# Second pass of a pooling and RWKV-7 trunk: projections of two blocks in one product, and part of the head moved into the inverse

## The chip, the cores and the metric

The kernel runs on one core of a Trainium2 chip. The metric is the device time of one execution in microseconds (us). The median of three executions of the kernel before is 2558.65 us, between 2556.53 and 2560.04.

## What is computed

The reference takes `x` of 4096 tokens by 1024 channels in float32 and one conditioning vector. Cut to what matters here:

```python
u = rms_norm(h, norm_gain) * (1 + scale) + shift
proj = u @ w_in                       # pool value, pool gate, r, k, v, w_down, a_down, rwkv gate
pf = p + (token_shift(p) - p) * mu    # on r | k | v | w_down | a_down
w_log = -softplus(-(w0 + tanh(wd) @ w_lora_up)) - 0.5;  decay = exp(-exp(w_log))
a = sigmoid(a0 + ad @ a_lora_up)
kk = l2_normalised(k * k_k);  k = k * (1 + (a - 1) * k_a)
# for each token, per head of 64 channels:
state = state * w_t + (state @ a_t) b_t^T + v_t k_t^T;  y_t = state @ r_t
y = group_norm(y) + (r * k * r_k).sum() * v
h = h + gate * (concat(y_pool * silu(...), y * silu(rg)) @ w_out)
out = rms_norm(h) * final_gain
```

The recurrence over tokens is what makes the second half of the kernel: tokens are taken in blocks, and inside a block the recurrence becomes products of small matrices and the inverse of a triangular one.

## The kernel before

All data are float32. A first pass computes the pooling branch and writes the transposed, normalised input to memory (`xt_dram`). The second pass, which the change touches, computes the RWKV branch in 32 blocks (`N2`) of 128 tokens (`T2`), each of two chunks of 64 tokens. A loop takes two blocks at a time (`each_block`, blocks 2 to 29), blocks 0 and 1 stand before it and 30 and 31 behind it.

**Queues.** Nothing is scheduled by a planner: each engine has its own queue, written out by hand in `run` (VectorE, ScalarE, GpSimd, SyncE) and in `front` and `back` (TensorE). Every engine works its queue strictly in order, and waits are on semaphores that count up per block.

**Projection.** The input of a block, `xT`, is 8 tiles of 128 channels by 128 tokens. 17 column tiles of weights are multiplied with it: tile 12 (low rank inputs), 0 to 3 (r), 4 to 7 (k), 8 to 11 (v), and 13 to 16 (the gate). Each tile takes 8 accumulated products (a float32 product shows as two records of MATMUL). They are put in five groups (`GROUPS`), which use PSUM banks 0 and 1 in turn. ScalarE copies a group out, scaled by `mu`, into `prev` (`take_group`, L1470), VectorE combines it with the bank to `mix` (`shift`, L1713), and only then may TensorE start the group after the next, which is what `mix_ready` tells it.

**Fillers.** The products of block n+1 are not run in a row: `project` is cut into 34 slots of four products, and `fill(k)` in `back` puts k slots of them between the small products of block n, so that TensorE has work while VectorE and ScalarE handle what the small ones gave. Inside the inverse (`inverses`, steps 0 to 5, L1276 and L1279) they use the full width of 128 weight columns (L1221). From step 5 on they are put as two halves of 64 columns (`halves`, L1202). The last six slots stand at the end of the block.

**The block's own work.** `front(n)` makes the variance of block n-1, the bonus, transposed values (L1364) and keys (`BT`, L1377), and the Gram matrices (L1386), for which it waits for VectorE's `LA` (L1851, L1857). Then `back(n)`: six slots, the inverse with the output product of block n-1 in two halves (L1256), and twice `from_state` (L1308), VectorE's copy `R` (L1793), `solve` (L1319), ScalarE's copy `UV`, and `state_and_output` (L1332, L1340, L1341). Behind the first of these VectorE sums the state (`stmp`, L1799) and makes the new one (`SV`, L1805).

**The head of block n+1** (low rank products L1232, sigmoid, key norm, decays `egi`, `sig`, `egx`, and `BK`) is worked behind the inverse of block n, between the state products, since its tiles are projected during that block.

**Loads.** SyncE issues for each block n: the load of `xT` for block n+2 (after the gate group of block n has been projected), the store of block n-1's output after `final_norm` (L1785), and, once that store has landed, the load of block n's residual rows (`gate_row`).

## Time and profile before

| | |
|---|---|
| median of three executions | 2558.65 us (2556.53 to 2560.04) |
| profiled execution | 2556.52 us, of which the core's span is 2553.4 us |
| TensorE busy, share of the span | 2484.1 us, 97% |
| VectorE, ScalarE, GpSimd busy | 65%, 45%, 17% |
| granted TensorE clock, mean | 0.988 |
| second pass | from about 659 us to the end |

Busy shares are of the whole span. A MATMUL's own duration includes its way through the array and overlaps with the next one; what a product costs in a row of products is therefore read from the distance between starts. An instruction's idle time is what its engine stood still before it, with the one that ended it.

### The profile page before, as it was taken

To read this page: it belongs to the slowest core of one execution; us is meant where nothing else is said; L and a number is where in the kernel's file an instruction comes from. 1 tells how busy PE (TensorE), PEld (TensorE's weight loads), DVE (VectorE), ACT (ScalarE), POOL (GpSimd) and SP (SyncE) were. 2 spreads that over 40 slices of the span, in tenths; PEclk is the share of its full clock that TensorE was granted. 3 is DMA by queue.
4 is the path that set the end of the run, shared out by engine and by line. 5 is a ranking of instruction groups with operands and counts; after the bars stand their busy time and mean duration, and the time that the engine had idled before them with its cause. 6 is when DMAs were issued, how large, how long until landed. Compare 5 with 4: busy or idle time off the path is not lost.

```text
span 2553.4 us, 73693 instructions
## 1 busy us (share of the span) xinstructions
PE 2484.1 (97%) x30485; PEld 2052.2 (80%) x30485; DVE 1660.4 (65%) x3462; ACT 1146.2 (45%) x2539; POOL 427.3 (17%) x565
## 2 busy tenths in 40 slices
PE   6999999999999999999999999999999999999995
PEld 6867776677678888888888888888888888888883
DVE  5653343433367777777777777677777776777774
ACT  4423322231235545444555545445555454455552
POOL 4211101111022111211111112111111111111110
PEclk8999999999999999999999999999999999999997
DMA  8513333126310100000100000000101000001000
GB/s 325 154 70 109 118 131 131 45 103 217 130 51 27 35 26 27 26 27 26 38 32 28 34 27 26 27 26 32 38 27 35 27 26 27 26 27 43 27 19 26
DMA packets 72618, 152.91 MB, mean 60 GB/s; under 512 B 3801, under 2 KB 38190, under 8 KB 71342
## 3 DMA queue, kind: packets, MB, share of 16 engines
q1 hardware_dynamic: 69918, 143.71, 16.0%
q8 instruction: 231, 3.78, 0.6%
q10 hardware_dynamic: 2448, 5.24, 0.6%
q14 instruction: 21, 0.17, 0.0%
HBM read 98.61 MB, written 50.33 MB: 58 GB/s over the span
## 4 chain that ended last, share of the span: by engine, by line
PE 85%; DVE 8%; ACT 4%; issue 3%; DVEq 0%; DMA 0%; SPq 0%; ACTq 0%
PE banks L1221 21%; PE banks L386 15%; PE banks L1202 13%; PE banks L1256 9%; PE banks L482 9%; PE banks L1276 7%; DVE SM L1868 2%; PE banks L1332 1%; PE banks L1386 1%; PE banks L1319 1%; PE banks L380 1%; PE banks L1340 1%; PE banks L1341 1%; PE banks L1308 1%; DVE t L1753 1%
## 5 line engine op out<-in xcount | busy, mean ns | idle before, releaser
L1221 PE MATMUL banks<-xT,wts 128*128 128x128 f32 x5232 | 633.7, 279 | 0.0
L1221 PEld LDWEIGHTS banks<-xT,wts 128*128 128x128 f32 x5232 | 598.3, 192 | 30.9 <-issue 27.1
L1531 ACT ACTIVATE LX<-banks 128x512 f32<-128x512 f32 (+1 forms) x384 | 184.9, 524 | 642.4 <-DVE WT L1812 436.3
L1202 PE MATMUL banks<-xT,wts 128*64 128x128 f32 x6944 | 420.1, 274 | 0.0
L1202 PEld LDWEIGHTS banks<-xT,wts 128*64 128x64 f32 x6944 | 380.2, 137 | 6.3
L1648 POOL TENSOR_TENSOR BK<-k,egi 64x512 f32<-64x512 f32 x64 | 96.3, 1504 | 928.3 <-ACT egi L1500 888.5
L1256 PE MATMUL banks<-wo,Y 128*128 128x512 f32 x512 | 232.9, 598 | 4.7 <-DVE Y L1772 4.7
L386 PE MATMUL banks<-ts,wts 128*128 128x256 f32 x1024 | 231.5, 379 | 0.0
L1812 DVE TENSOR_TENSOR WT<-banks,level_mask 128x256 f32<-128x256 f32 x256 | 102.5, 422 | 194.2 <-PE banks L1276 186.2
L482 PE MATMUL banks<-wo,yc 128*128 128x512 f32 x512 | 223.3, 595 | 0.0
L386 PEld LDWEIGHTS banks<-ts,wts 128*128 128x128 f32 x1024 | 194.9, 190 | 26.6
L482 PEld LDWEIGHTS banks<-wo,yc 128*128 128x128 f32 x512 | 96.8, 191 | 117.8 <-issue 117.7
L386 PE MATMUL banks<-xT,wts 128*128 128x256 f32 x768 | 180.1, 383 | 2.0 <-ACT xT L587 2.0
L1637 POOL TENSOR_TENSOR LA<-SM,ones 64x256 f32<-64x256 f32 x128 | 93.5, 730 | 529.3 <-DVE Y L1772 515.4
L1470 ACT ACTIVATE prev<-banks,vec 128x128 f32<-128x128 f32 x416 | 121.4, 374 | 121.9 <-PE banks L1221 114.1
L1256 PEld LDWEIGHTS banks<-wo,Y 128*128 128x128 f32 x512 | 93.5, 193 | 99.8 <-issue 94.3
L386 PEld LDWEIGHTS banks<-xT,wts 128*128 128x128 f32 x768 | 147.0, 192 | 26.2 <-issue 3.3
L1276 PEld LDWEIGHTS banks<-LX,W 64*64 64x64 f32 x4096 | 111.9, 134 | 58.0 <-issue 50.3
L1276 PE MATMUL banks<-LX,W 64*64 64x128 f32 x4096 | 143.1, 278 | 2.5 <-ACT LX L1531 1.5
L1713 DVE SCALAR_TENSOR_TENSOR mix<-banks,omu,prev 128x128 f32<-128x128 f32 x416 | 119.3, 345 | 26.0 <-ACT prev L1470 8.6
L873 DVE TENSOR_TENSOR fgain<-banks,fgain 128x256 f32<-128x256 f32 x96 | 40.7, 424 | 128.2 <-PE banks L386 127.4
L1840 DVE STREAM_TRANSPOSE WL<-banks 32x128 f32<-32x128 f32 x128 | 39.8, 311 | 126.8 <-PE banks L1276 123.8
(194 smaller groups left out, 3742.6 us busy)
## 6 DMA issues: line engine op xcount, KB each, us to landing
wo<-in_x SPq DMA_DIRECT2D x8, 2048.0 KB, 9.5
xt_dram<-xT SPq DMA_DIRECT2D x32, 512.0 KB, 8.4
xr<-in_x SPq DMA_DIRECT2D x32, 512.0 KB, 5.7
h_dram<-xr SPq DMA_DIRECT2D x32, 512.0 KB, 2.7
xT<-xt_dram SPq DMA_DIRECT2D x32, 512.0 KB, 3.4
gate_row<-h_dram SPq DMA_DIRECT2D x32, 512.0 KB, 3.4
out<-gate_row SPq DMA_DIRECT2D x32, 512.0 KB, 2.6
wts<-in_w_in SPq DMA_DIRECT2D x4, 2048.0 KB, 8.4
```

The lines of the kernel that those rows point to most:

```text
L386: last = nc.tensor.matmul(product_ps(g, i), w1[:, g, left, k], right[:, k], start=(k == 0), stop=(k == KH - 1))
L482: last = nc.tensor.matmul(bank[BANK_OUT[h]][:, :], yc[:, k, j * P:(j + 1) * P], wo1[:, k, h * 512:(h + 1) * 512], start=(k == 0), stop=(k ...
L1202: last = nc.tensor.matmul(o[half(c)], lhsT[:, half(c)], rhs, start=start, stop=stop)
L1221: last = (by_halves if halves else nc.tensor.matmul)(bank[b][:, q * P:(q + 1) * P], w2_tile(k, t0 + q), xT[par][:, k, :], start=(k == 0), ...
L1256: last = nc.tensor.matmul(bank[(4, 7)[h]][:, :], Y[:, p], wo2[:, p, h * 512:(h + 1) * 512], start=(p == 0), stop=(p == NP - 1))
L1276: last = nc.tensor.matmul(step_banks[a][half(c), j, p * P:(p + 1) * P], W[h, a, j, p], (LX if i else AI)[h, a, j, p].rearrange(flat), star ...
L1470: nx(nc.scalar.activation(prev[:, t, 1:], src, ACT.Copy, scale=v("mu", t)), mix_in, hold=False)
L1531: s(nc.scalar.activation(to, of, ACT.Copy), lx_ready, hold=False)
L1637: return nc.gpsimd.tensor_tensor(to, of, one, ALU.mult)
L1648: hd(nc.gpsimd.tensor_tensor(BK[h, :, :, 1 - e], chunks(k2[h]), chunks(egi[h]), ALU.mult), kt_ready if e else head_pool)
L1713: ins = nc.vector.scalar_tensor_tensor(out=mix[:, t], in0=bank[b][:, q * P:(q + 1) * P], scalar=omu[:, t:t + 1], in1=prev[:, t, 0:T2], op0 ...
L1812: s(nc.vector.tensor_tensor(WT[:, a], left(a)[:, :, 0:2, 0], mask_of(level_mask[i]), ALU.mult), wt_ready, hold=False)
```

## The change

Blocks are numbered as above; "an even block's projection" is the one that runs during the odd block before it.

- `xT` holds two blocks side by side, and the 13 tiles that go through `mix` are projected for two neighbouring blocks at once, 256 columns per product. Tiles 12, 4 to 9 are taken for blocks (2k+1, 2k+2) while block 2k runs; tiles 10, 0 to 3 and 11 for (2k, 2k+1) while block 2k-1 runs. The gate tiles stay at 128 columns. A group has at most two such tiles. Slots are now two products of 256 columns, or four of 128 for the gate: 36 and 32 slots.
- `fill(7)` stands where `fill(6)` stood.
- `prev` keeps only the two groups in flight. The last column of each tile is carried over in `carry` by small copies of ScalarE (three per group), and GpSimd's copy of that column goes.
- For even blocks, the low rank products, the key norm, the sigmoids and the decays move inside the inverse of the odd block before (`low_rank(0, (4, 7))`, `tanh`, `key(0)`, `clamp`, `decay_sum`, `taken_key`), and the final norm of the block before moves to the end of the odd block.
- `decay_ahead` and the exponential for `egx` go: `decay` has a leading column of ones, and serves both left sides. `dend` is copied from it.
- `xT` is loaded in two halves, each to rows of 512 bytes in SBUF that are 1024 bytes apart, where one load filled rows of 4096 bytes.
- The prologue projects the seven tiles of block 0 at 128 columns and the six others for blocks 0 and 1; block 31's seven are projected alone, at 128 columns.

```diff
-            GROUPS = [(12, 1, 0), (0, 4, 1), (4, 4, 0), (8, 4, 1), (13, 4, 0)]
+            GROUPS = ([(10, 1, 0), (0, 2, 1), (2, 2, 0), (11, 1, 1), (13, 4, 0)],
+                      [(12, 1, 0), (4, 2, 1), (6, 2, 0), (8, 2, 1), (13, 4, 0)])
+            GATE = 4
...
-                    sp.dma_start(xT[par][:, :, :], rows_of(xt, n)).then_inc(xT_loaded[par], 16)
+                    for h in range(2):
+                        k = slice(h * KH, (h + 1) * KH)
+                        sp.dma_start(xT[:, k, par, :], rows_of(xt, n)[:, k]).then_inc(xT_loaded[par][h], 16)
...
+                                for h in range(2):
+                                    pe.wait_ge(xT_loaded[par][h], (n - par) * 8 + 16)
+                                if seg is None:
+                                    pe.wait_ge(xT_loaded[1 - par][0], (n + par) * 8 + 16)
...
-                    fill(6)
+                    fill(7)
                     s.wait(bt_ready, 2)
-                    inverses(fill, (lambda h: None) if first else out_half, first)
+                    ahead_of = ahead and par == 1
+                    inverses(fill, (lambda: low_rank(0, (4, 7))) if ahead_of else (lambda: None),
+                             (lambda h: None) if first else (lambda h: out_half(h, ahead_of)), first)
+                    if ahead_of:
+                        key_norm()
                     from_state(0, first)
-                    if ahead:
-                        low_rank()
+                    if ahead and not ahead_of:
+                        low_rank(1)
...
+                    before, col = prev[:, b], carry[:, t0:t0 + w]
...
+                    nc.scalar.activation(before[:, 0:w, f, 0:1], col.unsqueeze(2), ACT.Copy)
                     for q in range(w):
-                        src = bank[b][:, q * P:(q + 1) * P]
-                        t = t0 + q
-                        nx(nc.scalar.activation(prev[:, t, 1:], src, ACT.Copy, scale=v("mu", t)), mix_in, hold=False)
+                        to, of = (before[:, q, :, 1:], both(b, q)) if seg is None else (before[:, q, seg, 1:], both(b, q, seg))
+                        ins = nc.scalar.activation(to, of, ACT.Copy, scale=v("mu", t0 + q))
+                    nx(ins, taken)
...
                     s.wait(y_ps, 1)
                     new_state(0, s, s_ready)
+                    if odd:
+                        decay_sum()
+                    if even:
+                        shift(n + 1, 1 - par, 2, seg)
+                    take_r(1)
+                    if odd:
+                        new_key(1)
+                    if even:
+                        new_key(0)
+                    state_sum(1)
+                    if even:
+                        decayed_key()
+                        if not first:
+                            final_norm(n - 1)
+                    if odd:
+                        taken_key()
                     if ahead:
-                        decay_sum()
-                    take_r(1)
+                        shift(n + 1, 1 - par, 3, seg)
```

(In the code `even` and `odd` speak of the block n+1 whose head is worked: `even` is true while an odd block runs.)

**TensorE, behind the inverse of an odd block.** Before, all blocks alike: step 5, a filler, `from_state` (L1308), low rank (L1232), `solve` (L1319).

```order
L1279 MATMUL banks<-LX,WL 64x64 x7
L1202 MATMUL banks<-xT,wts 64x128 x8
L1308 MATMUL banks<-SV,LA 64x64 [waits sv_ready,carried_ready,bt_ready,la_ready,lx_ready]
L1308 MATMUL banks<-SV,LA 64x64 x7
L1232 MATMUL banks<-th,up 128x128 [waits th_ready,mix_ready]
L1232 MATMUL banks<-mix,up 128x128
...
L1319 MATMUL banks<-R,LX 64x64 [waits r_ready]
L1319 MATMUL banks<-R,LX 64x64 x7
L1202 MATMUL banks<-xT,wts 64x128 x16
```

Now, in odd blocks:

```order
L1316 MATMUL banks<-LX,WL 64x64 x7
L1211 MATMUL banks<-xT,wts 64x256 x4
L1211 MATMUL banks<-rn,head_sum 64x512 [waits kk2_ready,lx_ready]
L1211 MATMUL banks<-rn,head_sum 64x512
L1347 MATMUL banks<-SV,LA 64x64 [waits sv_ready,bt_ready,carried_ready,la_ready]
L1347 MATMUL banks<-SV,LA 64x64 x7
L1358 MATMUL banks<-R,LX 64x64 [waits r_ready]
L1358 MATMUL banks<-R,LX 64x64 x7
L1211 MATMUL banks<-xT,wts 64x256 x8
```

The key norm stands ahead of `from_state` and the low rank products are gone from here, so `solve` follows `from_state` directly.

**TensorE, between the two chunks of an odd block, now.** The gate group opens the fillers behind the first `state_and_output` (L1380 is its last product).

```order
L1380 MATMUL banks<-LA,SV 64x64
L1211 MATMUL banks<-xT,wts 64x128 [waits mix_ready]
L1211 MATMUL banks<-xT,wts 64x128 x15
L1347 MATMUL banks<-SV,LA 64x64 [waits s_ready,v1_ready,la_ready]
L1347 MATMUL banks<-SV,LA 64x64 x7
```

Before, the fillers at this place needed no wait, and the gate group began two stops later, behind the second `solve`:

```order
L1202 MATMUL banks<-xT,wts 64x128 x16
L1202 MATMUL banks<-rn,head_sum 64x512 [waits kk2_ready]
L1202 MATMUL banks<-rn,head_sum 64x512
L1308 MATMUL banks<-SV,LA 64x64 [waits s_ready,v1_ready,la_ready]
L1308 MATMUL banks<-SV,LA 64x64 x7
L1202 MATMUL banks<-xT,wts 64x128 x8
L1319 MATMUL banks<-R,LX 64x64 [waits r_ready]
L1319 MATMUL banks<-R,LX 64x64 x7
L1202 MATMUL banks<-xT,wts 64x128 [waits mix_ready]
```

The gate group's wait has moved ahead of the second `from_state`.

**VectorE, the end of an odd block, now.** The first `mix` here is `shift(n + 1, ..., 2)`, the gate group's `mix_ready`; `gate_row` is the final norm of block n-1, after which its output may be stored.

```order
L1883 TENSOR_TENSOR stmp<-banks,SV 64x256 [waits s_ps,head_dve]
...
L1889 TENSOR_TENSOR SV<-stmp,dend 64x256 [waits y_ps,dve2_own]
...
L1800 SCALAR_TENSOR_TENSOR mix<-banks,omu,prev 128x256 [waits mix_in]
...
L1877 COPY R<-banks 128x256 [waits r_ps,mix_ready]
...
L1844 TENSOR_TENSOR BK<-rn,egi 64x8x64 [waits exps_ready,sum_ready]
L1844 TENSOR_TENSOR BK<-rn,egi 64x8x64
L1869 SCALAR_TENSOR_TENSOR gate_row<-gate_row,hstat,fgain 128x1024 [waits hn_ready]
...
L1800 SCALAR_TENSOR_TENSOR mix<-banks,omu,prev 128x256 [waits mix_in]
...
L1935 TENSOR_TENSOR LA<-mix,decay 64x8x64 [waits exps_ready,y_ps]
```

The same stretch before, without a final norm, which stood behind the first `R` and `rgate`:

```order
L1799 TENSOR_TENSOR stmp<-banks,SV 64x256 [waits s_ps,rk_ready]
...
L1752 TENSOR_TENSOR kk<-kk,rn 128x512 [waits rn_ready,sum_ready]
...
L1753 SCALAR_TENSOR_TENSOR t<-kk,sig 128x512 [waits head_dve]
...
L1713 SCALAR_TENSOR_TENSOR mix<-banks,omu,prev 128x128 [waits mix_in]
L1713 SCALAR_TENSOR_TENSOR mix<-banks,omu,prev 128x128 x3
...
L1760 TENSOR_TENSOR BK<-t,egi 64x8x64 [waits exps_ready]
L1760 TENSOR_TENSOR BK<-t,egi 64x8x64
...
L1851 TENSOR_TENSOR LA<-mix,sig 64x8x64 [waits exps_ready,y_ps]
```

The key work (`kk`, `t`) has left the end of the odd block and the final norm has come to it; `shift` of group 2 has come in behind the new state.

## Rows read from the trace of the kernel before

**Rows 1.** Stretches: length, busy us (count) of PE, PEld, DVE, ACT, POOL, clock, DMA

```profile
1000.00:2000.00 1000.00, 991.37 (x15244) 852.09 (x15240) 739.75 (x1635) 509.32 (x1196) 160.79 (x197) 1.00 0.09 29
```

**Rows 2.** Timeline of PE, one block: start, us, line, operation, count, idle before

```profile
1521.74 5.62 PE L1221 MATMUL banks<-xT,wts 128*128 128x128 f32 x48
...
1536.59 2.94 PE L1221 MATMUL banks<-xT,wts 128*128 128x128 f32 x24
1539.37 3.60 PE L1256 MATMUL banks<-wo,Y 128*128 128x512 f32 x8
...
1578.87 5.62 PE L1221 MATMUL banks<-xT,wts 128*128 128x128 f32 x48
```

**Rows 3.** Timeline of PE in the first pass, products of 256 columns

```profile
304.26 5.34 PE L386 MATMUL banks<-ts,wts 128*128 128x256 f32 x24
309.44 1.89 PE L386 MATMUL banks<-xT,wts 128*128 128x256 f32 x8
```

**Rows 4.** Timelines of PE, of DVE and of ACT, from inverse to state

```profile
1555.38 0.37 PE L1232 MATMUL banks<-th,up 64*128 64x128 f32 x1
...
1559.10 0.69 PE L1332 MATMUL banks<-UV,BT 128*64 128x64 f32 x16
...
1555.49 0.42 DVE L1793 COPY R<-banks 128x256 f32<-128x256 f32 x1 [1.72 <-PE banks L1308]
...
1561.47 0.87 DVE L1805 TENSOR_TENSOR SV<-stmp,dend 64x256 f32<-64x256 f32 x2
...
1556.16 1.14 ACT L1470 ACTIVATE prev<-banks,vec 128x128 f32<-128x128 f32 x4
...
1558.58 0.38 ACT L1536 ACTIVATE UV<-banks 64x256 f32<-64x256 f32 x1
```

**Rows 5.** Groups by form, 1000 to 2000 us: count, busy us, mean ns, idle

```profile
L1713 DVE SCALAR_TENSOR_TENSOR mix<-banks,omu,prev 128x128 f32<-128x128 f32 x226 | 64.9, 345 | 8.8
...
L1517 ACT ACTIVATE hstat<-hstat 128x1 f32<-128x1 f32 x17 | 3.4, 203 | 0.5
```

**Rows 6.** Timelines of DVE, then of PE, across a block's end

```profile
1498.92 1.28 DVE L1785 SCALAR_TENSOR_TENSOR gate_row<-gate_row,hstat,fgain 128x1024 f32<-128x1024 f32 x1 [0.15 <-ACT hstat L1517]
...
1510.65 0.88 DVE L1799 TENSOR_TENSOR stmp<-banks,SV 64x256 f32<-64x256 f32 x2 [0.23 <-PE banks L1332]
...
1512.29 1.66 DVE L1753 SCALAR_TENSOR_TENSOR t<-kk,sig 128x512 f32<-128x512 f32 x1
...
1518.21 1.41 DVE L1857 TENSOR_TENSOR LA<-kk,egx 64x512 f32<-64x512 f32 x2
...
1511.29 5.46 PE L1202 MATMUL banks<-xT,wts 128*64 128x128 f32 x96
1516.54 1.08 PE L1202 MATMUL banks<-rs,head_mean 128*64 128x512 f32 x4
...
1519.78 2.03 PE L1386 MATMUL banks<-LA,BK 64*128 64x128 f32 x32
```

**Rows 7.** Timeline of SyncE's queue

```profile
1500.36 0.36 SPq L1172 DMA_DIRECT2D out<-gate_row  x1
1504.54 0.33 SPq L1181 DMA_DIRECT2D gate_row<-h_dram  x1
...
1557.67 0.36 SPq L1172 DMA_DIRECT2D out<-gate_row  x1
1560.52 0.33 SPq L1181 DMA_DIRECT2D gate_row<-h_dram  x1
```

**Rows 8.** Issues of DMAs: KB each, median us to landing

```profile
xT<-xt_dram SPq DMA_DIRECT2D x32, 512.0 KB, 3.4
...
u<-in_pool_w ACTq DMA_DIRECT2D x1, 256.0 KB, 3.0
```

**Rows 9.** Timeline of PE: prologue of the second pass, and block 31

```profile
659.34 30.53 PE L1221 MATMUL banks<-xT,wts 128*128 128x128 f32 x272
...
2496.45 1.99 PE L1276 MATMUL banks<-AI,W 64*64 64x128 f32 x32 [5.45 <-DVE W L1824]
```

More of the change, by code:

```diff
@@ L1412, in back @@
                     fill(2, halves=True)
-                    if ahead:
+                    if ahead and not ahead_of:
                         key_norm()
@@ L1598, in run @@
                     take_y(0)
[L1599 removed]
+                    if odd:
                         sigmoid(1)
```

328 lines of the change are left out of this document (203 added, 125 removed).

## The prediction, made before the result was known

> **What bounds the kernel now.** I read the page's busy shares first, then the busy time by stretch, then TensorE's timeline over one block. TensorE is busy 97% of the span and 991.37 of 1000 us in the middle of the second pass, at full clock [rows 1]. The block shown lasts 57.13 us, 1521.74 to 1578.87 [rows 2]; the 17.5 blocks in those 1000 us share 8.6 us without work, 0.5 each. So time can be won only where TensorE's own work gets shorter, and any wait that is put before TensorE is paid in full. VectorE and ScalarE have idle time, but their chains of steps end exactly when TensorE asks for them: its Gram products begin at 1519.78, when the second `LA` ends at 1518.21 + 1.41 = 1519.62 [rows 6], and the state product begins at 1559.10, 0.14 us after the last `UV` [rows 4]. There is no slack that a new wait could use up.
>
> **What the wide product gives.** Distances of starts: full width at 128 columns, 1536.59 to 1539.37 for 24 records, 0.1158 us each. Two halves of 64 at 128 columns, 1511.29 to 1516.54 for 96, 0.0547 each, so 0.1094 for a pair [rows 2, 6]. At 256 columns, 304.26 to 309.44 for 24, 0.2158 [rows 3]. Twice 128 costs 0.2316 at full width and 0.2188 in halves. So a wide record saves 0.0158 at full width, nearly nothing in halves. No row shows halves at 256; I take 0.108 (half of 0.2158), between 0.107 and 0.109.
>
> Per pair of blocks before: 320 full-width records (20 of 34 slots per block), 37.06 us, and 448 half ones, 24.51: 61.57. After, 21 slots of each block are at full width and all are wide: 168 x 0.2158 = 36.25. In halves remain 8 gate slots per block, 256 x 0.0547 = 14.00, and 3 and 7 wide slots, 80 x 0.108 = 8.64. Sum 58.89, so **2.7 us less per pair**, and this is all that TensorE gains: the small products are the same in number.
>
> The Trainium skill (TensorE: Matmul & The Clock Gate, Back-to-back issue gap) gives N/2.4 + 2.5 ns for a warm gap, so hardly any gain from a wider product. With two passes over the columns for float32 it fits rows 3 (215.8) and the pairs of halves (109.2), but at full width and 128 columns the row has 115.8. By the page the gain per pair would be some 0.5 us and not 2.7, 32 us more over the kernel; the row of before decides.
>
> **What the new order puts before TensorE**, per pair of blocks.
>
> (a) *`solve` in odd blocks.* Low rank, 16 records from 1555.38 on, covers VectorE's `R` today. It moves away and nothing comes in its place. `R` ended at 1555.49 + 0.42 = 1555.91, 0.53 after `from_state`, and a release takes 0.14 (`UV` to L1332) [rows 4]. TensorE waits **0.7**.
>
> (b) *The gate group in odd blocks.* It opens the fillers right behind the first `state_and_output`, on the bank of group 2, so it waits for `mix_ready` of `shift(2)`. VectorE's queue has that behind the new state `SV`, which waits for `y_ps`, the end of the same `state_and_output`. TensorE stands for 0.11 (from its last product to VectorE's start, 1555.38 to 1555.49), 0.87 for `SV` [rows 4], two shifts and 0.14. A shift at 256 columns is not in the trace. Bounds are 0.345 at 128 and twice that; `R`, 256 columns from PSUM, takes 0.42 [rows 4, 5] and is nearest. I take 0.9 for two: **2.0** (1.8 to 2.5). The next product behind it, `from_state`, has what it needs by then, so nothing is given back.
>
> (c) *`xT` for the even block's run.* An even block's first filler now reads the load for the block two ahead as well. In SyncE's queue that load is behind the store of block n-1, which in odd blocks waits for a final norm moved to the block's end, and behind the residual load, which waits for that store to land. Count from the final norm's end, T. The store is issued 0.16 later (1498.92 + 1.28 to 1500.36), the residual load 2.85 or 4.18 after that [rows 6, 7], the first half of `xT` 0.4 later, at T + 3.4. An `xT` load of 512 KB lands 3.4 after its issue, one of 256 KB from elsewhere 3.0 [rows 8]; the residual load has 512 KB too. Landing is between T + 6.4 and, behind the residual's bytes, T + 7.7. TensorE asks at T + 5.7: shift 0.5, both `LA` (two like the row's, with gaps) 2.9, Gram products 1.96, gaps 0.3 [rows 2, 6]. Wait 0.7 to 2.0; I take **1.2**. The second half is asked for 1.7 later and lands in that time. What would cover it is nothing, since the slots ahead of the inverse all need this input. The load in rows of 512 bytes is not in the trace in this direction.
>
> The Trainium skill (DMA: Bandwidth & Descriptors, Anatomy of one DMA) has 2.0 us + bytes/436 KB per us, so 2.6 for a half, and 3.2 for 512 KB where the trace has 3.4; by it alone (c) would be 0.3 and the sum 14 us less.
>
> (d) *The end of odd blocks.* Six slots (1511.29 to 1516.54, 5.25) cover VectorE's chain from the end of `stmp` (1511.53) to that of the second `LA` (1519.62), 8.1 us. Now three gate slots, 2.6. The chain loses `kk` and `t`, which fill it up to 1513.95 (2.4), and some 0.6 of `mix`, and gains a final norm of 1.3: about 6.4. Filler shorter by 2.6, chain by 1.7: **0.8** (0.5 to 1.0) before bonus or Gram products [rows 6].
>
> (e) *ScalarE.* Before `UV` in even blocks ScalarE copied four tiles in 1.14 us [rows 4]. Now it makes two copies of 256 columns, the same columns in all with two fewer starts, some 0.9, and three small ones of 0.2 [rows 5]: 1.6. The state product followed `UV` by its release time, so it comes **0.5** later. In odd blocks the decays stand before the last step's copy, for which the key norm waits: **0.3**.
>
> Moving `tanh`, `clamp`, `key`, `decay_sum` into the inverse costs nothing: VectorE idles there under the output products and wide fillers. The dropped `egx`, its exponential, and GpSimd's carry shorten chains that only (d) reads.
>
> Sum per pair: 0.7 + 2.0 + 1.2 + 0.8 + 0.8 = 5.5 lost, 2.7 won, **+2.8**. The wide projections run in 15 pairs: +42 us.
>
> **Ends.** The prologue took 30.5 us for 272 records, 0.112 each [rows 9]. It gets 11 tiles at 128 columns (176 records, 19.7) and 6 at 256 (96, 20.7): +9.9, in the open. Block 30 then projects 6 tiles fewer (11.1 us of work), but its inverse is short of fillers; block 31, with none, stands 5.45 us before step 0 [rows 9]. I give back 4 (0 to 9). Together +6.
>
> **Sum.** 2556.52 (profiled) + 42 + 6 = 2604.5. The median of before is 2.1 above its profiled execution, so about **2605 us**, ratio 1.018.
>
> **Rivals.**
> - *The load is in time* (c = 0). For it: it may overlap the residual's. Against: the store must land first, which is 2.85 at least. 2605 - 18 = 2587.
> - *The load is much later*: 4.18 to the residual load or slow 512-byte rows, 2 us more per pair: 2635. One of three such distances seen in rows 7 and behind them was 4.18.
> - *Break-even*: (c), (d), (e) nearly nil, only (a) and (b) remain, which equal the gain: 2558 + 6 = 2564, or a little less.
> - *Faster*: the gate group does not wait. That needs `shift(2)` to be done before the fillers behind `state_and_output`; then VectorE is also 0.9 earlier for what follows, and (b), (d) vanish. With (a), (e), (c) at their low ends, 2.0 lost against 2.7, and the ends' 6 outweighed only if block 30 gives back 9: 2548. If all waits hid, 2556.5 - 40 + 6 = 2523. It decides at 2.3 us of waits per pair. Against it is the queue's order, in which `y_ps` stands ahead of that shift.
>
> **Chances.** Forecast 0.50 (2590 to 2622), load in time 0.18, load much later 0.12, break-even 0.08, faster 0.12. A difference of 0.2% (5 us) is about what can be told from no change. Slower by over 0.2%: 0.82; within: 0.06; faster: 0.12. The range 2560 to 2636 leaves out the faster case and the far end of the late load.
>
> **What would show it.** Starts of full-width wide records 0.216 apart. In odd blocks, TensorE idle some 0.7 before `solve` and some 2 before the first gate product, the releaser a `mix` of VectorE. In even blocks, idle before the first filler with a DMA or nothing named; a period of two blocks near 116.8 where it was 114.0, odd blocks longer than even ones in their middle. The forecast is wrong if TensorE is still 99% busy in the middle, if the gate product starts within 0.5 us of the state products, or if the pair is under 114.

## The result

The changed kernel takes **2674.47 us** (median of 5 runs, 2671.70 to 2686.11), the kernel before 2558.65 in the same comparison (5 runs). The ratio is 1.0472, 95% interval 1.0457 to 1.0486: slower by 116 us. The forecast was 2605 with a range of 2560 to 2636. The direction was right, the size was not: 46 us of loss were forecast, 2.5 times as much came.

The profiled execution of the changed kernel took 2686.11 us, with a span of 2684.4 and a mean granted clock of 0.971; it is the longest of the five, and the other four were granted 0.975 or 0.976. Its line numbers have moved: full-width fillers are L1251, fillers in halves and all other products by halves L1211, steps of the inverse L1313, the state product L1371, the Gram products L1425, VectorE's shift L1800.

The middle of the second pass, in the view that [rows 1] show for before (length, busy us and counts of PE, PEld, DVE, ACT, POOL, granted clock, DMA):

```profile
1000.00:2000.00 1000.00, 944.45 (x12108) 736.26 (x12109) 668.61 (x1394) 483.76 (x1212) 143.17 (x161) 0.98 0.08 27
```

TensorE is busy for 944 us where it was for 991, and the granted clock is 0.98 where it was 1.00. A clock that moved is the first thing for which the prediction had no term. TensorE's waits between 700 and 2600 us (total us, times, longest):

```profile
PE banks L1211 <- DVE mix L1800: 36.4, 26, 2.0
PE banks L1251 <- DMA xT<-xt_dram: 35.5, 15, 3.6
PE banks L1425 <- DVE LA L1940: 16.1, 16, 1.1
PE banks L1358 <- DVE R L1877: 10.3, 15, 0.7
PE banks L1371 <- ACT UV L1598: 5.2, 15, 1.0
```

All five were forecast by name, and four of them come once in each pair of blocks. The `mix` row holds two: the gate group's, 2.03 us in 15 pairs, and the bonus product's, 0.5 to 0.7 us in 11 of them. Together they are 6.8 us per pair.

TensorE's timeline, first an undisturbed run of fillers, then an odd block from the gate group on and the start of the next even block's run of fillers (start, us, in brackets the idle time before it and who ended it):

```profile
1530.94 6.31 PE L1251 MATMUL banks<-xT,wts 128*128 128x256 f32 x28
1537.19 1.10 PE L1313 MATMUL banks<-AI,W 64*64 64x128 f32 x32
...
1573.14 3.11 PE L1211 MATMUL banks<-xT,wts 128*64 128x128 f32 x32 [2.03 <-DVE mix L1800]
1576.03 1.07 PE L1347 MATMUL banks<-SV,LA 128*64 128x64 f32 x16
...
1578.63 1.97 PE L1211 MATMUL banks<-xT,wts 128*64 128x128 f32 x32
...
1586.07 1.09 PE L1211 MATMUL banks<-sig,rk_sum 128*64 128x128 f32 x16 [0.55 <-DVE mix L1800]
...
1589.50 2.06 PE L1425 MATMUL banks<-LA,BK 64*128 64x128 f32 x32 [1.06 <-DVE LA L1940]
1594.15 7.97 PE L1251 MATMUL banks<-xT,wts 128*128 128x256 f32 x28 [2.59 <-DMA xT<-xt_dram]
```

Not only the waits count here. The 32 records behind the gate group's wait need 2.89 us to the next product, where 32 such records at full clock need 1.80. The 28 wide records behind the load's wait need 7.90 (1594.15 to 1602.05), where the same 28 undisturbed need 6.25 (1530.94 to 1537.19). The stretches behind the two waits show why; the number behind POOL is the granted clock:

```profile
1574.00:1576.00 2.00, 2.00 (x22) 2.00 (x20) 0.00 (x0) 0.00 (x0) 0.00 (x0) 0.50 0.00 0
...
1594.00:1595.00 1.00, 0.85 (x2) 0.73 (x3) 0.88 (x2) 0.00 (x0) 0.00 (x0) 0.64 0.01 3
1595.00:1597.00 2.00, 2.00 (x6) 1.62 (x5) 1.90 (x6) 0.00 (x0) 0.00 (x0) 0.50 0.00 0
```

After standing still for 2.03 and for 2.59 us TensorE works at 0.50, which is 1.2 GHz, for some 3 us, and then again at 2.4 GHz. It does not follow every such wait, and that gives the price within one execution. The same place two pairs of blocks earlier, behind a wait of the same 2.03 us, with the granted clock at 1.00:

```profile
1329.60 1.97 PE L1211 MATMUL banks<-xT,wts 128*64 128x128 f32 x32 [2.03 <-DVE mix L1800]
...
1333.45 1.97 PE L1211 MATMUL banks<-xT,wts 128*64 128x128 f32 x32
...
1330.00:1333.00 3.00, 3.00 (x66) 2.83 (x64) 0.81 (x3) 0.00 (x0) 0.00 (x0) 1.00 0.00 0
```

From the gate group's first product to the second chunk's fillers it is 3.85 us here and 5.49 there (1573.14 to 1578.63): the lower clock costs 1.64. Behind the load's wait it costs as much: 7.90 for the run of 28, and 6.21 for the one behind a wait of 2.31 us at which the clock stayed up (1838.38 to 1844.59). In this execution the clock fell behind 13 of the 15 gate group's waits and 13 of the 15 load's waits (1.9 to 3.6 us).

From the first Gram products of block 1 to those of block 30 a pair takes 121.96 us (before 114.03, forecast 116.8). Block 0's Gram products begin at 742.30, before at 727.18. So the steady part lost 115 us, the prologue 15 and block 0 and the last two blocks together about 1, which is the difference of the spans, 131.

### The profile page after: what moved, and what is told of

Its sections match the earlier page's. It is cut to its first block, busy times and chain, and to the rows that moved or that the text cites. A ratio compares the mean times of both kernels' runs of the same rounds, so it can differ in the third digit from the quotient of the medians.

```text
span 2684.4 us, 65522 instructions
## 1 busy us (share of the span) xinstructions
PE 2517.2 (94%) x26409; PEld 1940.3 (72%) x26409; DVE 1624.5 (61%) x3229; ACT 1152.8 (43%) x2694; POOL 421.5 (16%) x534
## 4 chain that ended last, share of the span: by engine, by line
PE 84%; DMA 5%; DVE 5%; ACT 4%; issue 2%; SPq 1%; POOL 0%; DVEq 0%; ACTq 0%; POOLq 0%
PE banks L1251 24%; PE banks L386 15%; PE banks L1211 13%; PE banks L1293 8%; PE banks L482 8%; PE banks L1313 6%; DMA xT<-xt_dram 2%; DMA out<-gate_row 1%; PE banks L1371 1%; PE banks L1358 1%; PE banks L1425 1%; PE banks L1347 1%; DMA xT<-in_w_ada 1%; DVE BK L1844 1%; PE banks L1379 1%
## 5 line engine op out<-in xcount | busy, mean ns | idle before, releaser
L1251 PE MATMUL banks<-xT,wts 128*128 128x256 f32 (+1 forms) x2876 | 668.3, 387 | 38.5 <-DMA xT<-xt_dram 35.5
L1251 PEld LDWEIGHTS banks<-xT,wts 128*128 128x128 f32 x2876 | 529.7, 197 | 135.5 <-issue 65.2
L1211 PE MATMUL banks<-xT,wts 128*64 128x128 f32 (+1 forms) x5224 | 406.5, 308 | 30.4 <-DVE mix L1800 30.4
L1211 PEld LDWEIGHTS banks<-xT,wts 128*64 128x64 f32 x5224 | 320.3, 142 | 63.2 <-DVE mix L1800 32.5
L386 PEld LDWEIGHTS banks<-xT,wts 128*128 128x128 f32 x768 | 147.4, 192 | 26.3 <-issue 3.3
L1313 PEld LDWEIGHTS banks<-LX,W 64*64 64x64 f32 x4096 | 112.0, 134 | 68.1 <-issue 66.1
L1313 PE MATMUL banks<-LX,W 64*64 64x128 f32 x4096 | 143.2, 278 | 2.5 <-ACT LX L1593 1.6
L1524 ACT ACTIVATE prev<-carry 128x2 f32<-128x2 f32 (+1 forms) x132 | 28.1, 213 | 258.0 <-PE banks L1251 223.6
L1908 DVE STREAM_TRANSPOSE W<-WT 128x256 f32<-128x256 f32 x320 | 121.7, 418 | 0.0
L1800 DVE SCALAR_TENSOR_TENSOR mix<-banks,omu,prev 128x256 f32<-128x256 f32 (+1 forms) x215 | 94.6, 472 | 37.6 <-ACT prev L1530 15.7
```

The lines of the kernel that those rows point to most:

```text
L386: last = nc.tensor.matmul(product_ps(g, i), w1[:, g, left, k], right[:, k], start=(k == 0), stop=(k == KH - 1))
L1211: last = nc.tensor.matmul(o[half(c)], lhsT[:, half(c)], rhs, start=start, stop=stop)
L1251: last = one(to, w2_tile(k, t0 + q), x, start=(k == 0), stop=(k == KT - 1))
L1313: last = nc.tensor.matmul(step_banks[a][half(c), j, p * P:(p + 1) * P], W[h, a, j, p], (LX if i else AI)[h, a, j, p].rearrange(flat), star ...
L1800: ins = nc.vector.scalar_tensor_tensor(out=mix[:, t, of], in0=both(b, q)[:, of], scalar=omu[:, t:t + 1], in1=prev[:, b, q, of, 0:T2], op0= ...
L1908: s(nc.vector.transpose(W[:, a].rearrange("p j q t -> p (j q t)"), WT[:, a].rearrange("p j q t -> p (j q t)")), w_ready, hold=False)
```

## The experiments

Theory A: the changed kernel loses by the waits in TensorE's queue that its new order makes, and by a granted clock that falls behind the two long ones. Rivals: each product costs more than it did (the width, or the traffic beside it); TensorE is slow after a wait for another reason than the clock; or the load is slow in itself. Every ratio is against the kernel before on the same chip in the same comparison. Differences between two versions are differences of medians, mostly from two comparisons; the kernel before had medians between 2554.7 and 2558.65 in them, so such a difference is good to about 4 us.

### The gate group's shift earlier

Odd blocks only; on VectorE the shift stands ahead of the state's sum and not behind the new state:

```diff
                     elif ahead:
                         shift(n + 1, 1 - par, 2, seg)
...
+                    if even:
+                        shift(n + 1, 1 - par, 2, seg)
                     state_sum(0)
...
                     new_state(0, s, s_ready)
-                    if even:
-                        shift(n + 1, 1 - par, 2, seg)
```

> The changed kernel with one thing moved: in odd blocks VectorE does the shift of group 2 ahead of the state sum, not behind the new state, so that the gate group's wait (2.03 us per odd block in the changed kernel's trace) should go. Theory A (the clock: a wait of 2 us of TensorE is followed by products at half the granted clock, which costs as much again): the wait and the slow stretch behind it both go, 2.0 + 1.7 us in 15 pairs, 55 us, so about 2619 us. Theory B (the slow products behind the waits are slow for another reason, such as contention or their own width): only the wait goes, 30 us, so about 2644 us, and the gate products between the two chunks still show 0.09 us each. Theory C (the waits only move): under 10 us.

Measured: 2632.95 us, ratio 1.0299 (1.0282 to 1.0317), 41.5 less than the changed kernel. The gate group's wait is gone, the rest stands:

```profile
PE banks L1251 <- DMA xT<-xt_dram: 32.6, 15, 3.6
...
PE banks L1211 <- DVE mix L1800: 9.6, 15, 0.7
```

Of the 41.5 us, 30.4 are the wait (15 times 2.03). The other 11 us, 14 by the ratios, fit the clock: at 1.64 for a fall they are 7 or 8 falls fewer in 15 pairs of a common run. That number is an estimate, since only the longest execution of the changed kernel has a trace, and it shows 13. The load's waits stayed, and the clock fell behind 11 of those 15.

### The load earlier

SyncE issues both loads ahead of the odd block's store. The last blocks' calls are written out so that no load goes past the end.

```diff
-                def run(n, first, ahead, par):
-                    if ahead == 2:
-                        load_xT(n + 2, par)
+                def run(n, first, loads, par):
+                    if par:
+                        if loads:
+                            load_xT(n + 2, 1)
+                        if loads == 2:
+                            load_xT(n + 3, 0)
+                    elif first:
+                        load_xT(n + 2, 0)
```

> The changed kernel with SyncE's order changed alone: in odd blocks the input load for the next block stands ahead of the store that waits for the final norm, where it stood behind it and behind the residual load. The wait before an even block's first filler (2.3 us, 35.5 in 15) should go. Theory A (clock): that wait and the seven slots behind it at half clock (7.97 us where full clock takes 6.3) both go, 2.3 + 1.7 in 15 pairs, 60 us, so about 2614 us. Theory B (other reason for the slow slots): 35 us, so about 2640 us, the slots still at 7.97. If the load is late for its rows of 512 bytes and not for its place in the queue, the wait stays: about 2674.

Measured: 2622.04 us, ratio 1.0254 (1.0237 to 1.0271), 52.4 less than the changed kernel. The `xT` wait falls from 35.5 us to one of 2.3. So 33 us are the wait, and the other 19 fit the clock again. Of the gate group's waits, all of them 1.95 to 2.04 us as before, 7 of 15 are followed by a fall here.

> Both of the above in one. Theory A: both waits and both slow stretches go, 115 us, so about 2560 us, and the clock stays at its upper level throughout the second pass: what is left over the kernel before is the prologue and the small waits. Theory B: 65 us, about 2610 us. If the wide products were worth the 2.7 us per pair that was forecast, 2540 to 2550 us; if they are worth the 1.4 us read from the trace of after (0.223 us per record), 2560 us or a little above.

Measured with both edits together: 2582.62 us, ratio 1.0104 (1.0087 to 1.0121), 91.9 less; the two gains are additive within 2 us (41.5 + 52.4 = 93.9), within 6 by the ratios. The granted clock between 1000 and 2000 us is 1.00 again:

```profile
1000.00:2000.00 1000.00, 976.03 (x12970) 762.06 (x12968) 716.21 (x1482) 517.88 (x1294) 155.60 (x172) 1.00 0.09 28
```

Two moved instructions take back four fifths of the loss. What is left, 26 us, is about the short waits (2.7 per pair) and the prologue, less the product's gain and the waits of the kernel before that are gone.

### A wait alone, in the kernel before

Is it the clock, or does something else in the changed kernel slow the products behind a wait? Into the kernel before goes a wait and nothing else, behind the first `state_and_output`:

```diff
                     state_and_output(0, first)
+                    if ahead:
+                        nx.wait(G_ready, 1)
                     fill(2, halves=True)
```

> The kernel before with one wait put in: behind the first state_and_output of every block with a block ahead, TensorE waits for VectorE's running sum of decays, some 2.2 us after its last product, in 31 blocks; nothing wide is in it. Theory A (clock): the fillers behind that wait run at half the granted clock for some microseconds, as in the changed kernel; 31 x (2.2 + 1.5 to 2) = 115 to 130 us, so 2675 to 2690 us. Theory B: the clock stays up, 31 x 2.2 = 68 us at most, so about 2625 us.

Measured: 2700.20 us, ratio 1.0561 (1.0543 to 1.0578), 144 more. TensorE's timeline and the stretches behind one of the waits:

```profile
1504.23 3.06 PE L1202 MATMUL banks<-xT,wts 128*64 128x128 f32 x32 [2.91 <-DVE G L1737]
...
1505.00:1506.00 1.00, 1.00 (x13) 1.00 (x10) 0.00 (x0) 0.09 (x1) 0.00 (x0) 0.50 0.00 0
```

There is no wide product, no late load and no new order here, and the pattern is the same: 31 waits of 2.7 to 2.9 us are 88 us, and 56 us more, 1.8 for each, come with them, at 1.2 GHz behind every one of the 31. With the pairs of equal waits in the changed kernel, one with a fall and one without, that settles the clock. The same with a short wait:

```diff
-                        nx.wait(G_ready, 1)
+                        s.wait(s_ready, 1)
```

> The kernel before with one wait added at the same place as in e4_before_wait, but a short one: behind the first state_and_output TensorE waits for the new state (s_ready), one step of VectorE, and not for G. In e4 waits of 2.9 us cost 90 us by themselves and 54 more, at a granted clock that fell behind each. Theory A, 'short waits cost their length alone' (in e3_both waits up to 1.1 us left the granted clock at 1.00): 31 waits of 1.1 us, 34 us more, 2590, granted clock as in before. Theory B, 'any wait on this stretch costs clock': the next 32 records take 2.8 and not 1.75 here too, 34 + 31 x 1.7 = 87 more, 2643.

Measured: 2614.34 us, ratio 1.0232 (1.0218 to 1.0246), 59 more, between the two expectations. The timeline tells why:

```profile
PE banks L1202 <- DVE SV L1807: 49.0, 31, 1.6
...
1526.99 0.34 PE L1341 MATMUL banks<-LA,SV 128*64 128x64 f32 x4
1528.87 1.97 PE L1202 MATMUL banks<-xT,wts 128*64 128x128 f32 x32 [1.54 <-DVE SV L1807]
1530.67 1.03 PE L1202 MATMUL banks<-rn,head_sum 128*64 128x512 f32 x4
...
1529.00:1530.00 1.00, 1.00 (x20) 1.00 (x21) 1.00 (x1) 0.94 (x4) 0.00 (x0) 1.00 0.56 168
```

The wait is 1.54 us here and 1.64 in every other block, since the new state comes that much later, and not 1.1: 31 of them are 49 of the 59 us. Behind none of the 31 did the granted clock leave 1.00, and the 32 records take 1.80. So theory A holds in what tells the two apart. Most of the 10 us beside the waits is how a wait is counted: idle time begins when the last product has ended, and without a wait the next one starts before that. From the start of the last state product to that of the fillers it is 1.88 us (1526.99 to 1528.87), in the kernel before 0.12 (1560.40 to 1560.52), so a wait shown as 1.54 costs 1.76, and 31 of them cost some 56 us. In the same way some 0.2 of e4's 1.8 are the wait's own. With e3_both's steady part (waits up to 1.1 us, clock 1.00) the rows say: up to 1.65 us a wait cost its length and up to 0.2, from 1.9 on it often cost 1.6 more. The length alone does not decide: behind waits of 2.03 us the clock fell in 13 of 15 cases in the changed kernel's trace, in 7 in e2's, in 4 in e8's. What else decides stays open.

### The final norm and the queue's order

One part of the change undone: the final norm of odd blocks, and the residual's norm on ScalarE, go back to where they were.

```diff
-                    if not first and not even:
+                    if not first:
                         final_norm(n - 1)
...
                     if even:
                         decayed_key()
-                        if not first:
-                            final_norm(n - 1)
```

> The changed kernel with one part undone: the final norm of odd blocks (and the residual's norm on ScalarE) stand where they stood before, behind R, and not at the block's end. The store and the residual load are then issued some 13 us earlier, so xT's load is in time. Theory A, 'the place of the final norm makes the xT wait and most of the wait at the block's end, and each long wait costs clock as well': xT's wait goes (2.3 x 15), the waits at the end (bonus and LA, 1.6) fall by about 1.3, and with xT's wait goes the low clock behind it (some 1 us per pair): 15 x 4.6 = 69 less, 2605. Theory B, 'the load is slow itself or its bank of buffers is late': the xT wait stays, only 1.3 x 15 go, 2655. The gate group's wait stays in both.

Measured: 2600.03 us, ratio 1.0167 (1.0153 to 1.0181), 74 less than the changed kernel, as theory A said. Waits:

```profile
PE banks L1211 <- DVE mix L1798: 30.4, 15, 2.0
...
PE banks L1425 <- DVE LA L1938: 5.0, 14, 0.8
```

`xT`'s wait and the bonus product's are gone, LA's fell from 1.06 to 0.36 us. The gate group's wait, 2.03 us in 15 pairs, stays. This one move, 1.28 us of VectorE's work put at the block's end, carries the largest part of the loss: 53 us are waits, the other 21 fit the clock, which falls behind 4 waits in this trace and behind 26 in the changed kernel's. Why was the load's wait 2.3 and not the 1.2 of the forecast? The next kernel leaves the late norm and store, but puts the even block's load ahead of the residual load:

```diff
                         store(n - 1)
+                        if par and loads == 2:
+                            load_xT(n + 3, 0)
                         let_through(sp, sp_gate)
                     sp.dma_start(hr[:, :], rows_of(h1_t, n)).then_inc(h_loaded, 16)
```

> The changed kernel with one part of SyncE's queue changed: xT's load for the even block stays behind the store (and so behind the late final norm), but is issued ahead of the residual load and not behind it. In after, counted from the final norm's end, the residual load was issued at 3.1, xT at 4.2, and TensorE's first filler began at 8.8, where it had asked at 6.5. Theory A, 'the residual load ahead of it made the wait so long' (its issue 1.1, and its bytes, behind which the half took 4.5 us instead of 3.2 as elsewhere): issue at 3.1, landing at 6.3 to 6.6, the wait falls from 2.3 to 0 to 0.3, and no clock falls there: 15 x (2.2 + 1.2) = 51 less, 2623. Theory B, 'the load in 512-byte rows is slow behind any store': landing 4.5 behind its issue, at 7.6, wait 1.1, 15 x 1.2 to 15 x 2.4 less: 2638 to 2656.

Measured: 2634.29 us, ratio 1.0310 (1.0296 to 1.0324), 40 less than the changed kernel. SyncE's queue and the landings (KB each, median us from issue), first in the changed kernel, where the final norm ended at 1585.31:

```profile
1585.49 0.37 SPq L1181 DMA_DIRECT2D out<-gate_row  x1
1588.39 0.35 SPq L1190 DMA_DIRECT2D gate_row<-h_dram  x1
1589.51 0.95 SPq L1176 DMA_DIRECT2D xT<-xt_dram  x2
...
xT<-xt_dram SPq DMA_DIRECT2D x2, 256.0 KB, 4.5
```

and in this kernel, where it ended at 1562.06:

```profile
1562.25 0.37 SPq L1181 DMA_DIRECT2D out<-gate_row  x1
1565.28 0.94 SPq L1176 DMA_DIRECT2D xT<-xt_dram  x2
1566.46 0.34 SPq L1195 DMA_DIRECT2D gate_row<-h_dram  x1
...
xT<-xt_dram SPq DMA_DIRECT2D x2, 256.0 KB, 3.5
...
PE banks L1264 <- DMA xT<-xt_dram: 7.9, 9, 2.5
```

Issued 1.0 us earlier after the norm and landing 1.0 faster, the load keeps TensorE waiting for 7.9 us in all where it was 35.5. So the residual load ahead of it made the wait: through SyncE's time, 1.12 from one issue to the next where the forecast had 0.4, and through its 512 KB. The time is 11 above theory A's: the wait gave back 28 us where 33 were expected, and what goes with the clock 13 where 18 were.

### Covering the last waits

From e3_both on: the key norm between `from_state(0)` and `solve(0)`, the final norm of odd blocks behind the second R, ScalarE's copy of group 2 ahead of the key's scale and the residual's norm behind the first UV, `shift(2)` right behind the first R, `shift(3)` ahead of BK.

```diff
-                    if ahead_of:
-                        key_norm()
                     from_state(0, first)
+                    if ahead_of:
+                        key_norm()
...
                     if even:
+                        if not first:
+                            final_norm(n - 1)
                         new_key(0)
                     state_sum(1)
-                    if even:
-                        decayed_key()
-                        if not first:
-                            final_norm(n - 1)
...
                     if ahead:
                         shift(n + 1, 1 - par, 3, seg)
-                    if odd:
+                    if ahead:
                         decayed_key()
```

> The version of e3_both with its last waits in odd blocks attacked: the key norm stands between from_state(0) and solve(0), so it covers VectorE's R; the final norm of odd blocks stands behind the second R and not at the block's end; ScalarE copies group 2 ahead of the key's scale and does the residual's norm behind the first UV; shift(3) stands ahead of BK. Theory A, 'the new order's waits are all that is left': R's wait (0.7 x 15), the bonus product's (0.65 x 15) and most of LA's (1.06, of which 0.4 stays) vanish, 33 us less, 2550. Theory B, 'VectorE's chain at the block's end is full anyway': the final norm delays the new key and BK by what it frees behind them, only R's wait goes, 2572.

Measured: 2553.80 us, ratio 0.9990 (0.9981 to 0.9999), 29 less than e3_both and level with the kernel before. R's and the bonus product's waits are gone and LA's has halved:

```profile
PE banks L1384 <- ACT UV L1611: 7.7, 18, 1.0
PE banks L1438 <- DVE LA L1951: 7.7, 16, 0.8
```

The last step leaves one more slot for the odd block's end and lets ScalarE take UV first in even blocks:

```diff
-                        fill(3 if i < LV else 2)
+                        fill(3 if i < LV - (par == 1 and ahead == 2) else 2)
...
-                    if odd:
-                        exp_low_rank(0)
                     if even:
                         key_scale()
                     take_u(0)
+                    if odd:
+                        exp_low_rank(0)
```

> The version of e7_cover with two changes: in odd blocks one filler slot less is issued behind step 3 of the inverse, so that one more (0.86 us) is left for the block's end; in even blocks ScalarE takes UV ahead of the first exponential of the low rank. e7_cover still stood 7.7 us in 16 waits for LA and 5.7 in 16 for UV between 700 and 2500. Theory A, 'only waits are left between the new order and its gain': both go, some 0.5 + 0.3 per pair, 15 pairs: 12 less, 2542, ratio 0.995. Theory B, 'the slot was needed inside the inverse': the last factor or step waits by as much there, 2550 to 2560.

Measured: 2544.83 us, **ratio 0.9955 (0.9941 to 0.9968)**: faster than both kernels. LA's wait is down to one of 0.8 us, in the first block, UV's to three. A pair takes 112.10 us against 114.03 before. That is 28 us over the steady part, of which the longer prologue takes back 17. Not all of it is the products: the kernel before stood 0.52 us per pair for VectorE's `W` and for `UV`, and these waits are gone, while one of 0.16 for the key norm has come.

### The width by itself

How much of that is the width? The schedule of e9_one_slot_later stays, but each full-width wide product becomes two of 128 columns:

```diff
-                        last = one(to, w2_tile(k, t0 + q), x, start=(k == 0), stop=(k == KT - 1))
+                        if gr != GATE and seg is None and not halves:
+                            for j in range(2):
+                                last = one(both(b, q, j), w2_tile(k, t0 + q), xT[:, k, j],
+                                           start=(k == 0 and j == 0), stop=(k == KT - 1 and j == 1))
+                        else:
+                            last = one(to, w2_tile(k, t0 + q), x, start=(k == 0), stop=(k == KT - 1))
```

> The version of e9_one_slot_later with one thing undone: each full-width wide product (256 columns of x, 84 per block) is written as two of 128 columns, one for each block's half, so that the schedule of the change stays and only the width goes. Theory A, the prediction's price (0.2316 for two narrow records against 0.2158, the rest equal): 168 x 0.0158 = 2.7 us per pair come back, 40 us in all: 2585. Theory B, from the runs of products in these traces (0.1177 a narrow record and 0.05 a run of them, 0.2163 a wide one and 0.195 a run, 12 runs per pair): 3.2 - 1.7 = 1.5 us per pair, 22 us: 2567. Theory C, that the product's width brings nothing here: 2545.

Measured: 2560.39 us, ratio 1.0019 (1.0010 to 1.0028), which is 0.0064 or 16 us above e9. A pair takes 113.21 us, 1.11 more than in e9, whose trace holds one late load of 1.9 us that e12's does not; without it the distance is 1.24. TensorE's timeline, with wide products (e9):

```profile
1530.06 6.31 PE L1264 MATMUL banks<-xT,wts 128*128 128x256 f32 x28
1536.30 1.10 PE L1326 MATMUL banks<-AI,W 64*64 64x128 f32 x32
1537.33 2.86 PE L1264 MATMUL banks<-xT,wts 128*128 128x256 f32 x12
1540.12 1.10 PE L1326 MATMUL banks<-LX,W 64*64 64x128 f32 x32
```

and with narrow ones (e12):

```profile
1529.20 6.52 PE L1266 MATMUL banks<-xT,wts 128*128 128x128 f32 x56
1535.65 1.10 PE L1330 MATMUL banks<-AI,W 64*64 64x128 f32 x32
1536.68 2.94 PE L1266 MATMUL banks<-xT,wts 128*128 128x128 f32 x24
1539.56 1.10 PE L1330 MATMUL banks<-LX,W 64*64 64x128 f32 x32
```

From a run's start to the next step's products: 6.24 and 2.79 us for 28 and 12 wide ones, 6.45 and 2.88 for 56 and 24 narrow ones, and behind them in the block 1.93 for 8 wide and 1.98 for 16 narrow. The wide ones fit 0.2156 for a record and 0.20 for each run; two narrow ones 0.2232, and the same 0.20 for each run. In the kernel before, 24 and 16 took 2.87 and 1.98 likewise (its 48 took 5.70 to 6.00, but there the step waits for VectorE's `W`). So, by this fit, a run of fillers pays some 0.2 us where a step's products end it, whatever the width, and a wide record saves 0.0076. The width saves 0.21 + 4 x 0.09 + 0.05 = 0.6 per block, 1.2 per pair, 18 us in 15 pairs, against 16 measured. The expectation's theory B had the price of a run wrong (0.05 narrow, 0.195 wide) and is nearest all the same.

Can the full-width products be made cheaper as halves? In the changed order (the edit shown) and in the kernel before, where the same choice is made in its own line:

```diff
-                    one = nc.tensor.matmul if not halves else by_halves
+                    one = nc.tensor.matmul if prologue else by_halves
```

> The version of e3_both with one change: the wide products at full width (256 columns, 84 records per block) are written as two halves of 64 columns of weights. Theory A, 'a fixed cost per run of products': in the trace of after, runs of 28, 12 and 8 wide full-width records take 6.25, 2.79 and 1.93 us to the next step's first record, which fits 0.216 a record and 0.19 for each run, while 8 and 16 wide records in halves take 0.92 and 1.73 to 1.77, which fits 0.108 a record and about 0.05 a run. Then halves save some 0.14 for each of 6 runs per block, 0.8 us per block, 25 us in all, and the time is about 2558. Theory B, 'each wide record is dearer in the second pass' (0.223, for instance through the other engines' traffic): two halves would be dearer likewise or equal, and the time stays at 2583, or goes up where twice the instructions cost issue time.

> The kernel before with one change: the fillers at full width (128 columns, 160 records per block) are written as two halves. In before, runs of 48, 24 and 16 full-width records take 5.70, 2.87 and 1.98 us (0.118 a record, 0.05 a run), 96 half records 5.25 (0.0547 each). Theory A: halves are cheaper, 0.1094 for two against 0.118, so 160 records save 1.1 to 1.3 us per block, of which the first run's 0.45 only lengthens the wait for the first factor; 0.8 x 31 gives 2530 (2520 to 2540). Theory B: the chains on VectorE and ScalarE set the pace, nothing is won, 2556. Theory C: 160 more instructions per block cost issue time: 2570 or more. By A the gain of the wide product must be measured against 0.1094, so that it is nothing; by B or C the full-width price stands.

Measured: 2590.18 us, ratio 1.0130 (1.0111 to 1.0148), 7.6 more than e3_both; and 2550.95 us, ratio 0.9983 (0.9974 to 0.9992), 5 less than before. Neither gives what was expected of theory A; both are nearer to theory B, by which halves win nothing or lose. In e6, 48 half records take 2.77 us wherever they stand. That is 0.1 less than the 2.87 of 24 full ones ahead of a step, but no less than their 2.78 ahead of an output product, and the output product itself then takes 3.70 and not 3.60:

```profile
1533.16 2.84 PE L1202 MATMUL banks<-xT,wts 128*64 128x128 f32 x48
1535.93 3.70 PE L1256 MATMUL banks<-wo,Y 128*128 128x512 f32 x8
```

So the 0.1 us that halves save at the end of a run comes back in the output product behind them. Why is not shown; that going over from one shape of product to another has a price would fit.

## Why the forecast was right in direction and too low in size

The waits were found where they are, and they outweigh the gain, so the direction was no luck. Two steps of the sum failed. It priced every wait of TensorE at its length alone and so put the granted clock at nothing, where it cost some 30 us. And it took 2.7 us per pair for the wide product, where the runs give 1.2, which is 21 us. The sizes of (c), (d) and the ends, each too low, make most of the rest.

**The product's gain, 2.7 us per pair: measured 1.2.** It set a record of a run of 24 narrow ones in the second pass, 2.78 / 24, against one of 24 wide ones in the first pass that another wide stream follows. The first quotient holds the end of the run (part of the 0.20), the second doesn't. Like for like, run by run with the same product behind it, the width gives 1.2 (e12), and 168 records at 0.0076 give 1.3. The halves were priced right: 16 wide ones took 1.73 us, 0.108 each. The estimate of 0.5 that was weighed against this row, from a formula of the Trainium skill (TensorE: Matmul & The Clock Gate, Back-to-back issue gap) that the page gives for a single matmul by itself, is too low; the measurement lies between the two.

**(a) `solve` without cover, 0.7:** measured 0.69 in each odd block, with R as releaser. **(b) The gate group, 2.0:** measured 2.03. The queue on VectorE was read rightly, down to the shift at 256 columns (0.87 for two against 0.9 taken). e1 took it away and no other wait came in its place.

**(c) The load, 1.2:** measured 2.3. The mechanism was right, a store behind the late final norm and two loads behind it. Two sizes were not: the issue after the residual load's (1.12, not 0.4) and the landing (4.5 us, not 3.0 to 3.4; in e11, alone behind a store, 3.5). TensorE also asked 0.5 us later than forecast, 6.25 after the norm's end and not 5.7, which took some of it back. The formula of the Trainium skill (DMA: Bandwidth & Descriptors, Anatomy of one DMA), which the page fits to DMAs issued from GpSimd, gives 2.6 for such a half; for these loads, issued from SyncE, the trace doesn't agree, with 3.2 in e3_both, where they are issued ahead of the store.

**(d) The odd block's end, 0.8:** measured 1.5, 1.06 ahead of the Gram products in each pair and some 0.55 ahead of the bonus product in 11 of 15. The cover was 2.63 as forecast. VectorE's chain, from the end of `stmp` to that of the second `LA`, was forecast at 6.4 and is 7.4 us:

```profile
1581.18 0.88 DVE L1883 TENSOR_TENSOR stmp<-banks,SV 64x256 f32<-64x256 f32 x2 [0.94 <-PE banks L1371]
1582.09 1.91 DVE L1844 TENSOR_TENSOR BK<-rn,egi 64x512 f32<-64x512 f32 x2
1584.03 1.28 DVE L1869 SCALAR_TENSOR_TENSOR gate_row<-gate_row,hstat,fgain 128x1024 f32<-128x1024 f32 x1
...
1586.60 1.41 DVE L1935 TENSOR_TENSOR LA<-mix,decay 64x512 f32<-64x512 f32 x2 [0.68 <-DVE mix L1800]
```

`BK` takes 1.91 where it takes 1.43 before: it begins at 1582.09, while GpSimd's own half of `BK` runs from 1579.68 for 3.05 us. In [rows 6] it was `t`, 1.66, that paid for this; with `t` gone the price stayed. It was counted as saved.

**(e) ScalarE, 0.8:** UV's wait is 0.30, where the kernel before had 0.15; the key norm's isn't there.

**The clock, not priced at all.** The prediction named a wait of 2.0 us and one of 1.2 and took both at their length. e1 gave 11 us beside the wait, e2 19: together 30. The kernel before has no such wait in its steady part, and of the rows shown ahead of the prediction only block 31's has one (5.45), without the clock beside it. But its trace has one in the prologue, with the fall behind it:

```profile
693.73 1.60 PE L1202 MATMUL banks<-rn,head_sum 128*64 128x512 f32 x4 [2.77 <-ACT rn L1491]
...
695.00:697.00 2.00, 2.00 (x4) 0.84 (x3) 1.00 (x3) 1.63 (x3) 0.00 (x0) 0.50 0.01 4
```

So the price of a long wait could have been looked for before the change. The Trainium skill (TensorE: Matmul & The Clock Gate, HAM oscillation) tells of a kernel in which each wait for a load of some 3 to 5 us is followed by products at the lower clock. The traces agree in kind, and show it behind waits of 1.9 to 2.9 us too, though not behind each.

**The ends, 6:** measured 16. The prologue's products take 45.6 us instead of 30.5. They account for 10 as forecast; two waits for `mix` (1.94 and 1.02) add 3, and the clock behind the first (0.50 from 666 to 669) some 1.7. Block 30 gave back 3.7, as taken.

**The sum, by medians:** waits 6.8 x 15 = 102, less some 7 of the kernel before that vanished; clock 30; products -19; ends 16. That is 122, where 116 were measured; the clock's 30 and the ends' 16 are the least certain of these terms, the ends being from the longest execution. The rival "load much later", 2635, was the nearest one, and even it lacked the clock. e8 shows the rival "load in time" with its own reason: 2600, against 2587 forecast. "Faster" was wrong as the change was built. That a version with the waits gone is faster was right, but by 0.45% and not by the 1.4% of its arithmetic (2523), which held the 2.7.

## What to carry to other kernels

Price a wait of TensorE by its length only while it is short; the rows here add some 1.6 us to one of 1.9 us or more, not each time; up to 1.65 us they add 0.2 at most. Between the two no wait was measured. Compare two forms of a product only between runs that have the same length and the same product behind them. And when a step moves to a queue's end, follow every DMA that waits for it up to the instruction that waits for the last landing: here a norm of 1.3 us was worth 74.

## What the runs showed of the hardware that was not expected

- The granted clock fell to 0.50 behind single waits of 1.9 to 3.6 us and came back about 3 us later; behind 31 waits of 1.4 to 1.65 us it stayed at 1.00 (e10). It fell behind all 31 waits of 2.7 to 2.9 in e4, and behind those of 2.03 in 13 of 15 cases (changed kernel), 7 of 15 (e2) and 4 of 15 (e8). A fall cost 1.64 us: 5.49 against 3.85 for the same products behind the same wait.
- A run of products ended by an inverse's step cost some 0.2 us beyond its records, at 128 as at 256 columns; output products behind halves took 3.70 us, behind full-width ones 3.60.
- A VectorE product that began while a GpSimd product ran on the same core ended some 0.55 us after it: the first of the two `BK` took 1.29 us for its 0.69, with GpSimd's end 0.75 after its start, and `t` before 1.65, with 1.10. `sig<-mix,k`, which began 0.13 us ahead of GpSimd's product, took its usual 0.69, and so did `stmp`, with one input in PSUM, its usual 0.42.
